# Neighbourhood scores of two query tiles per run of 64-row matmuls, and the reciprocals' transpose behind the odd unit's turning

## What is computed

```python
def neighbourhood_attention(q, k, v, rpb):      # q, k, v: b, 4 heads, s, 64
    ...
    scores = jnp.einsum('bhrcqe,bhrcke->bhrcqk', qg, kg,
                        preferred_element_type=jnp.float32) * (hd ** -0.5)
    ...
    scores = scores + bias[None].astype(jnp.float32)
    p, _ = masked_softmax(scores, col_ok)
    out = jnp.einsum('bhrcqk,bhrcke->bhrcqe', p.astype(v.dtype), vg,
                     preferred_element_type=jnp.float32)

def encoder_layer(x, ...):
    hn = rmsnorm(x, g_pre_mix)
    proj = hn @ w_in
    ...
    y_dil = dilated_attention(qd, kd, vd)        # three (window, dilation) branches, combined
    y_na = neighbourhood_attention(qn, kn, vn, rpb)
    y_conv = short_conv_mixer(gate_b, gate_c, h_in, conv_w)
    mixed = jnp.concatenate([y_dil, y_na, y_conv], axis=-1) @ w_out
    x = x + rmsnorm(mixed, g_post_mix)
    hf = rmsnorm(x, g_pre_ffn)
    f = (jax.nn.silu(hf @ w_gate) * (hf @ w_up)) @ w_down
    return x + rmsnorm(f, g_post_ffn)
```

## Time and profile before

| | us |
|---|---|
| median of 3 runs | 2976.72 |
| lowest and highest of them | 2976.03, 2982.83 |
| the profiled execution, device time | 2978.13 |
| its span in the profile | 2976.3 |
| PE busy in the span | 2945.0 |
| DVE busy | 2025.8 |
| ACT busy | 1225.3 |
| POOL busy | 933.2 |

### The profile page before, as it was taken

The page is one execution under the profiler, slowest core; times in us unless marked ns, Lnnn a source line. Parts: engine busy times, 40 slices in busy tenths (PEclk is TensorE's granted clock), DMA queues, the critical chain, the costliest instruction groups (busy, mean ns, idle before and its releaser), DMA issues.

```text
span 2976.3 us, 50329 instructions
## 1 busy us (share of the span) xinstructions
PE 2945.0 (99%) x19328; PEld 2786.9 (94%) x19328; DVE 2025.8 (68%) x3695; ACT 1225.3 (41%) x2377; POOL 933.2 (31%) x762
## 2 busy tenths in 40 slices
PE   9999999999999999999999999999999999999998
PEld 8888887999999999999988888879999999999998
DVE  7977856388744447687888778563886444476786
ACT  5434444453422225444554444444534222254342
POOL 1211212755622225001542012137555222350013
PEclk9999999999999999999999999999999999999999
DMA  4111012333222225644531110313232222257345
GB/s 159 43 54 60 22 64 83 116 117 112 86 86 70 71 72 188 223 128 155 183 102 51 51 58 15 102 60 132 96 126 82 70 70 70 88 173 258 97 144 198
DMA packets 153452, 307.53 MB, mean 103 GB/s; under 512 B 16129, under 2 KB 76161, under 8 KB 152961
## 3 DMA queue, kind: packets, MB, share of 16 engines
q1 hardware_dynamic: 148784, 291.74, 30.0%
q10 hardware_dynamic: 4432, 12.58, 1.1%
HBM read 238.73 MB, written 57.67 MB: 100 GB/s over the span
## 4 chain that ended last, share of the span: by engine, by line
PE 89%; DVE 6%; issue 2%; POOL 1%; ACT 1%; DMA 1%; SPq 0%; ACTq 0%; DVEq 0%; POOLq 0%
PE PS L2843 26%; PE PS L2845 26%; PE PS L2844 25%; PE PS L3009 3%; PE PS L2993 3%; PE PS L2977 2%; PE PS L2965 1%; PE PS L2881 1%; POOL OSS L1393 1%; DVE ACCUM L2162 1%; DVE PT L2588 1%; DVE ACCUM L2154 0%; PE PS L2937 0%; DVE PR L2541 0%; PE PS L3018 0%
## 5 line engine op out<-in xcount | busy, mean ns | idle before, releaser
L2843 PE MATMUL PS<-XH,WH 128*128 128x512 f32 (+1 forms) x1152 | 431.8, 375 | 8.8 <-DVE VD L2433 2.8
L2845 PE MATMUL PS<-XH,WL 128*128 128x512 f32 (+1 forms) x1152 | 409.6, 356 | 0.0
L2844 PE MATMUL PS<-XL,WH 128*128 128x512 f32 (+1 forms) x1152 | 408.2, 354 | 0.0
L1421 POOL TENSOR_TENSOR GL<-GR,GH 128x512 fp32r<-128x512 f32 x186 | 251.5, 1365 | 366.4 <-ACT GH L1788 304.3
L2843 PE MATMUL PS<-DHH,DWH 128*128 128x384 f32 (+1 forms) x1056 | 328.3, 311 | 0.0
L2845 PE MATMUL PS<-DHH,DWL 128*128 128x384 f32 (+1 forms) x1056 | 326.6, 309 | 0.0
L2844 PE MATMUL PS<-DHL,DWH 128*128 128x384 f32 (+1 forms) x1056 | 325.8, 309 | 0.0
L2843 PEld LDWEIGHTS PS<-XH,WH 128*128 128x128 f32 x1152 | 217.4, 189 | 60.1 <-issue 21.5
L2845 PEld LDWEIGHTS PS<-XH,WL 128*128 128x128 f32 x1152 | 217.3, 189 | 32.2
L2844 PEld LDWEIGHTS PS<-XL,WH 128*128 128x128 f32 x1152 | 218.0, 189 | 24.4
L2844 PE MATMUL PS<-CL0T,GH 128*128 128x384 f32 x704 | 238.4, 339 | 0.0
(11 more groups left out here) (271 smaller groups left out, 8341.1 us busy)
## 6 DMA issues: line engine op xcount, KB each, us to landing
GR<-w_gu SPq DMA_DIRECT2D x62, 768.0 KB, 4.2
RAW<-w_in SPq DMA_DIRECT2D x48, 512.0 KB, 3.7
DHR<-hidden SPq DMA_DIRECT2D x66, 320.0 KB, 4.4
DWR<-w_down SPq DMA_DIRECT2D x66, 256.0 KB, 3.7
S3B<-w_down SPq DMA_DIRECT2D x66, 256.0 KB, 3.4
GR<-w_gu SPq DMA_DIRECT2D x62, 256.0 KB, 2.8
T3B<-hidden SPq DMA_DIRECT2D x44, 320.0 KB, 4.0
hidden<-S1T SPq DMA_DIRECT2D x44, 192.0 KB, 1.9
```

The source lines that it names most:

```text
L1421: nc.gpsimd.tensor_tensor(GL[v % 2][:, m, :, :], GR[v % 2][:, m, :, :], GH[v % 2][:, m, :, :].bitcast(F32), ALU.subtract).then_inc(s_wlo_r ...
L2843: nc.tensor.matmul(out, wh, xh, start=first, stop=False, skip_group_check=reopened)
L2844: nc.tensor.matmul(out, wh, xl, start=False, stop=False, skip_group_check=reopened)
L2845: return nc.tensor.matmul(out, wl, xh, start=False, stop=last, skip_group_check=reopened)
```

## The change

In the neighbourhood blocks (`b not in DIL`) an odd pair's scores go to banks 1 and 3 instead of 0 and 2, so two pairs' scores exist at once. `scores(0)` and `scores(1)` stand together ahead of the unit loop; units 2, 6, 10 and 14 each issue two pairs, and units 0, 4, 8, 12 and 16 none. An odd pair waits only for the masks of the pairs up to two before it. In all blocks `spread_recip` of a pair moves from behind the fill of the even unit to behind `turn` of the following odd unit, and on DVE `y` moves from ahead of the odd unit's low part to behind it. ACT's exponential of an even unit from 4 on waits for POOL's copy of the pair whose sums it overwrites.

```diff
--- before.py
+++ after.py
@@ -1711,6 +1711,8 @@
                 def exp(u):
                     i, h, k0, nkt = units[u]
                     act.wait_ge(s_masked, first + u + 1)
+                    if u >= 4 and u % 2 == 0:
+                        act.wait_ge(s_recip, NP * nb + u // 2 - 1)
                     nc.scalar.activation(PR[:, u % 2, 0:nkt * P], PR[:, u % 2, 0:nkt * P], ACT.Exp,
                                          scale=-1.0, bias=NM[:, u % 4:u % 4 + 1],
                                          accum_out=SM[:, u % 4:u % 4 + 1]).then_inc(s_exped, 1)
@@ -2523,6 +2525,8 @@
                     if b in DIL and i < 8:
                         mask_halves(u, ps)
                         return
+                    if b not in DIL:
+                        ps = PS[:, 2 * (u % 2) + u // 2 % 2, :]
                     nc.vector.tensor_tensor_reduce(PR[:, u % 2, 0:nkt * P], ps[:, 0:nkt * P],
                                                    table(i, h, nkt), -1.0, 3e38, ALU.add, ALU.min,
                                                    NM[:, u % 4:u % 4 + 1]).then_inc(s_masked, 1)
@@ -2578,8 +2582,6 @@
                 drain(*last_cover)
                 split_v(nb, slice(4, None))
                 for u in range(NU):
-                    if u > 1 and u % 2:
-                        y(u // 2 - 1)
                     if u and u % 2 == 0:
                         add_parts(u // 2 - 1)
                     for g, (a, n) in enumerate(quads(units[u][3])):
@@ -2589,6 +2591,8 @@
                             parts_of(b, u)[:, 1, a:a + n, :].rearrange("p t q -> p (t q)"),
                             PS[:, 4 + g, 0:n * P], high.bitcast(F32), ALU.subtract) \
                             .then_inc(s_ptl, 1)
+                    if u > 1 and u % 2:
+                        y(u // 2 - 1)
                     if u + 2 < NU:
                         mask(u + 2)
                     if u % 2:
@@ -2946,8 +2950,9 @@
                 def scores(pair):
 
                     i, _, k0, nkt = units[2 * pair]
-                    if pair:
-                        pe.wait_ge(s_masked, first + 2 * pair)
+                    side = pair % 2 if b not in DIL else 0
+                    if pair > side:
+                        pe.wait_ge(s_masked, first + 2 * pair - 2 * side)
                     if pair in (0, 4, 8):
                         pe.wait_ge(s_stack_lo, STACK_LO[(L, "k", b, 1) if pair == 0 else (L, "q", b, pair // 4)])
                     if b in DIL and i < 8:
@@ -2962,7 +2967,7 @@
                             else:
                                 half, block = divmod(i, COL_BLOCKS)
                                 keys = grid_keys(k, block, half, KEY_TILES)[own, :, :]
-                            last = nc.tensor.matmul(PS[:, 2 * h, 0:nkt * P], q[own, i * P:(i + 1) * P], keys,
+                            last = nc.tensor.matmul(PS[:, 2 * h + side, 0:nkt * P], q[own, i * P:(i + 1) * P], keys,
                                                     start=m == 0, stop=m == 2)
                             if m == 2:
                                 last.then_inc(s_scored, 1)
@@ -3036,6 +3041,8 @@
                 cover(L, b, 1)
                 pe.wait_ge(s_vl, V_BASE[nb] + min(4, len(v_groups(b))))
                 scores(0)
+                if b not in DIL:
+                    scores(1)
                 cover(L, b, 2)
                 if b not in DIL:
                     pe.wait_ge(s_yb, 2 * NP * nb)
@@ -3044,14 +3051,17 @@
                     if u and u % 2 == 0:
                         values(u // 2 - 1)
                     turn(u)
-                    if u % 2 == 0 and u + 2 < NU:
+                    if u > 1 and u % 2:
+                        spread_recip(u // 2 - 1)
+                    if b in DIL and u % 2 == 0 and u + 2 < NU:
                         scores(u // 2 + 1)
+                    if b not in DIL and u % 4 == 2 and u + 2 < NU:
+                        scores(u // 2 + 1)
+                        scores(u // 2 + 2)
                     fill(u)
                     if b == LAST and u in (NU - 3, NU - 2):
                         pe.wait_ge(s_masked, NU * nb + NU - 1)
                         output_group(L, 0, 0, range(2) if u == NU - 3 else range(2, 4))
-                    if u and u % 2 == 0:
-                        spread_recip(u // 2 - 1)
                 if b != LAST:
                     cover(L, b + 1, 0, range(4))
                 else:
```

## The result

| | us |
|---|---|
| kernel before, median of 8 runs | 2977.92 |
| changed kernel, median of 8 runs | 2987.61 |
| ratio, 95% interval | 1.0034 [1.0025, 1.0043] |
| span of the profiled execution, before and after | 2976.3, 2985.1 |

The change costs 9.7 us in the medians and 8.8 us in the spans; +6.2 was forecast. The point lies just beyond the 0.3% that the chances were split at, on the slower side, which had been given 0.28; the interval lies on both sides of that bound.

A forecast was written before the change was run, and what follows sets the result against it. The matmul engine, busy 2945.0 of 2976.3 us, was taken as the bound. Waits in neighbourhood blocks (+5.3 us) and later `y` in dilated blocks (+0.9) gave +6.2, or 2982.9 us against the 2976.72 median; range 2973 to 2991.

The forecast's parts named there:

- the 0.3% that the chances were split at: Whole kernel: what a measurement tells from no change, about 0.3% or 8.9 us; bounds 2967.8 and 2985.6 us.
- the slower side: Whole kernel: slower than 2985.6 us, chance 0.28, of which 0.12 is the upper end of the forecast.

## What to carry to other kernels

Work that is taken out of a busy engine's stream at one place is worth its time only if the chain through the other engines ends before what is left there. Write down, for each unit, the length of that chain beside the engine's remaining work, and deal out the movable work again together with the edit. And when a short operation is moved behind another, follow the whole queue behind it to the next two hand-overs, not only to the first.

## What the runs showed of the hardware

- VectorE's multiplication of 128x512 with both inputs in SBUF took 0.68 us alone and 2.74 us when it started just after GpSimd's subtraction of 128x1024 (2.37 us). In the traces of before and after, all 14 such multiplications that started during such a subtraction ended 0.55 us after it, whenever they had started (one that started late took only 1.44 us, at 51.84 us of after). The two that started just ahead of a subtraction kept 0.68 us (249.11 and 1727.88 us of before), and the subtraction took 2.77 and 2.68 us. So the later one got almost nothing done until the earlier one was through. That the two share a path to SBUF is argued from this, not shown.
- VectorE's low parts of 128x512, which have one input in PSUM, took 0.67 to 0.69 us with the same subtraction beside them (ten in the trace of before) and without it.
- In a run of twelve 64-row matmuls, from the second pair of heads on, each starts 0.18 us after the last through a change of weights and of query tile; entering and leaving the run cost 0.36 us once.
